# Division of softmax probabilities moved from VectorE to GpSimd in a two-layer streaming encoder

## The reference, cut to what matters

```python
def sink_softmax(s, sink):
    m = jnp.maximum(jnp.max(s, axis=-1, keepdims=True), sink)
    e = jnp.exp(s - m)
    return e / (jnp.sum(e, axis=-1, keepdims=True) + jnp.exp(sink - m))
...
    s = jnp.einsum('nbqhgd,nbkhd->nbhgqk', qb, kb).astype(jnp.float32) * ATTN_SCALE
    p = sink_softmax(s, sink)
    o = jnp.einsum('nbhgqk,nbkhd->nbqhgd', p.astype(v.dtype), vb)
```

## Time and profile before

| | before |
|---|---|
| median of 3 runs | 2451.64 us |
| profiled execution, its own time | 2451.63 us |
| span of that execution, first to last instruction | 2450.4 us |
| mean granted TensorE clock | 0.995 |
| busy: TensorE / VectorE / ScalarE / GpSimd | 2396.0 / 1652.9 / 842.4 / 109.6 us |
| chain that ended last, share of TensorE / VectorE | 92% / 4% |
| attention, first turn to last values, layer 0 | 209.42 to about 276 us |

### The profile page before, as it was taken

One profiled execution on the slowest core, in us unless ns is written; L12 is line 12 of the kernel. 1 busy time (PEld: TensorE's weight loads), 2 busy tenths in 40 slices (PEclk: granted clock), 3 DMA queues, 4 the chain that ended last, 5 costly groups with the idle time before them and its releaser, 6 DMA issues.

```text
span 2450.4 us, 45650 instructions
## 1 busy us (share of the span) xinstructions
PE 2396.0 (98%) x17474; PEld 2354.0 (96%) x17474; DVE 1652.9 (67%) x2472; ACT 842.4 (34%) x1602; POOL 109.6 (4%) x199
## 2 busy tenths in 40 slices
PE   6999999999999999999999999999999999999997
PEld 6997899999999999999999978999999999999996
DVE  8888888875435663645788888888754366556376
ACT  4126422223423432423431273222243244334243
POOL 0023100000000000000000231000000000000000
PEclk9999999999999999999999999999999999999998
DMA  4221122222232222222232201222222322222223
GB/s 182 86 86 37 36 84 85 79 78 78 95 98 87 78 86 78 77 86 78 88 122 79 94 19 60 77 86 77 81 83 92 102 86 78 85 78 86 78 82 105
DMA packets 57367, 204.22 MB, mean 83 GB/s; under 512 B 8142, under 2 KB 8238, under 8 KB 57006
## 3 DMA queue, kind: packets, MB, share of 16 engines
q1 hardware_dynamic: 52560, 190.03, 23.1%
q0 software_dynamic: 4704, 12.79, 1.8%
HBM read 193.14 MB, written 8.50 MB: 82 GB/s over the span
## 4 chain that ended last, share of the span: by engine, by line
PE 92%; DVE 4%; issue 1%; ACT 1%; DMA 0%; DVEq 0%; ACTq 0%; SPq 0%
PE ps L493 85%; PE ps L522 5%; PE ps L588 1%; DVE w_lo L1026 1%; ACT w_hi L760 1%; PE ps L573 1%; DVE scratch L1279 1%; PE ps L605 1%; PE ps L533 0%; DVE score_max L1252 0%; PE ps L590 0%; DVE scratch L1268 0%; DVE branch_lo L1287 0%; DVE scratch L1040 0%; DVE x_q_merged L1518 0%
## 5 line engine op out<-in xcount | busy, mean ns | idle before, releaser
L760 ACT ACTIVATE w_hi<-raw 128x1024 fp32r<-128x1024 f32 x348 | 368.9, 1060 | 1231.2 <-PE ps L493 1161.3
L493 PE MATMUL ps<-xn_hi,w_hi 128*128 128x296 f32 (+1 forms) x3584 | 779.1, 299 | 2.6 <-DVE w_lo L1026 2.6
L493 PE MATMUL ps<-xn_hi,w_lo 128*128 128x296 f32 (+1 forms) x3584 | 778.8, 299 | 0.0
L493 PE MATMUL ps<-xn_lo,w_hi 128*128 128x296 f32 (+1 forms) x3584 | 774.3, 297 | 0.0
L1026 DVE TENSOR_TENSOR w_lo<-raw,w_hi 128x1024 fp32r<-128x1024 f32 x350 | 428.7, 1225 | 494.1 <-ACT w_hi L760 493.0
L493 PEld LDWEIGHTS ps<-xn_hi,w_hi 128*128 128x128 f32 x3584 | 583.2, 189 | 4.3 <-DVE w_lo L1026 2.7
L493 PEld LDWEIGHTS ps<-xn_lo,w_hi 128*128 128x128 f32 x3584 | 582.8, 189 | 0.0
L493 PEld LDWEIGHTS ps<-xn_hi,w_lo 128*128 128x128 f32 x3584 | 579.8, 189 | 0.0
L493 PE MATMUL ps<-branch_hi,w_hi 128*128 128x296 f32 (+1 forms) x1296 | 282.7, 299 | 0.4
L493 PE MATMUL ps<-branch_hi,w_lo 128*128 128x296 f32 (+1 forms) x1296 | 281.6, 299 | 0.0
L493 PE MATMUL ps<-branch_lo,w_hi 128*128 128x296 f32 (+1 forms) x1296 | 279.9, 297 | 0.0
(11 more groups left out here) (160 smaller groups left out, 2173.3 us busy)
## 6 DMA issues: line engine op xcount, KB each, us to landing
raw<-in_weights SPq DMA_DIRECT2D x350, 512.0 KB, 3.2
spill<-x_q_merged POOLq DMA_DIRECT2D x2, 2368.0 KB, 9.3
x_q_merged<-spill POOLq DMA_DIRECT2D x16, 296.0 KB, 3.1
x_q_merged<-in_xt SPq DMA_DIRECT2D x4, 592.0 KB, 8.1
out_y<-x_q_merged SPq DMA_DIRECT2D x8, 296.0 KB, 2.3
scratch<-scratch POOLq DMA_DIRECT2D x64, 18.5 KB, 2.8
con<-in_consts SPq DMA_DIRECT2D x1, 592.0 KB, 11.3
vec<-in_vecs SPq DMA_DIRECT2D x1, 576.0 KB, 5.6
```

The lines of the kernel that those rows point to most:

```text
L493: last = nc.tensor.matmul(out[:, h, :], a[:, s, wk], b[:, k, t0 + h * n:t0 + (h + 1) * n], start=(k == 0 and j == 0), stop=(k == nk - 1 an ...
L760: nc.scalar.activation(wh[:, s, :], raw[:, s, :], ACT.Copy).then_inc(hi_done, 1)
```

## The change

The division leaves VectorE. GpSimd does it for all 20 units of a layer, in a new function `divide`, and its order becomes stage(0,0), stage(0,1), then for each chunk n: stage(n+1,0), divide(n,0), stage(n+1,1), divide(n,1). Each divide waits for its reciprocal and for the two copies ahead of it; each stage waits for the divide ahead of it. GpSimd's loop over the chunks is written out. On VectorE, denominators(n-1,1), now only the sum and the reciprocal, stands ahead of copy_rest(n-1,0), and the reciprocal waits until the division of the chunk before has read the old one. TensorE's transposes wait for the same semaphore as before, now raised by GpSimd. The nine DMAs after the last stage now also stand behind the last two divisions.

```diff
+            def divide(n, v):
+
+                nk = chunk_span(n)[2]
+                pool.wait_ge(rinv_done, l * 20 + n * 2 + v + 3)
+                pool.wait_ge(p_done, l * 20 + n * 2 + v + 3)
+                pool.wait_ge(qs_done, l * 20 + min(n * 2 + v + 3, 20))
+                plain()
+                probs = view(O_P + 768 * v, 768).rearrange("p (i n) -> p i n", i=4)[:, :, 0:nk]
+                nc.gpsimd.tensor_tensor(probs, probs, rinv[:, v, :].rearrange("p (i o) -> p i o", o=1)
+                                        .to_broadcast([128, 4, nk]), ALU.mult).then_inc(pn_done, 1)
+
+            for v in range(N_KV):
+                stage(0, v)
+            for n in range(CHUNKS):
                 for v in range(N_KV):
...
+                    if n + 1 < CHUNKS:
+                        stage(n + 1, v)
+                    divide(n, v)
...
-            pe.wait_ge(pn_done, it + 1)
+            pe.wait_ge(pn_done, it + 3)
...
             def denominators(n, v):
-                nk = chunk_span(n)[2]
                 it = l * 20 + n * 2 + v
                 dve.wait_ge(p_done, it + 3)
                 V.tensor_tensor(sums[:, v, :], sums[:, v, :], es[:, v, :], ALU.add).then_inc(den_done, 1)
                 dve.wait_ge(den_done, it + 1)
+                dve.wait_ge(pn_done, it + 1)
                 V.reciprocal(rinv[:, v, :], sums[:, v, :]).then_inc(rinv_done, 1)
-                dve.wait_ge(rinv_done, it + 3)
-                probs = view(O_P + 768 * v, 768).rearrange("p (i n) -> p i n", i=4)[:, :, 0:nk]
-                V.tensor_tensor(probs, probs, rinv[:, v, :].rearrange("p (i o) -> p i o", o=1).to_broadcast([128, 4, nk]),
-                                ALU.mult).then_inc(pn_done, 1)
...
                 if has(n - 1):
+                    denominators(n - 1, 1)
                     copy_rest(n - 1, 0)
-                    denominators(n - 1, 1)
```

More of the change, by code:

```diff
@@ L368, in plain @@
             nc.gpsimd.sem_inc(carrier, 1)
+        nc.gpsimd.sem_inc(pn_done, 2)
         pool.dma_start(vs[:, 0:WINDOW - DEC_SEQ, :], vcache[:, DEC_SEQ:WINDOW, :]).then_inc(vs_out, 16)
@@ L412, in _ @@
                     partners(m % 2)
-            def stage(c, n):
-                q0 = chunk_span(c)[0]
-                for v in range(N_KV):
[L418 to L434, removed]
+            def stage(n, v):
+                q0 = chunk_span(n)[0]
+                if n == 0:
+                    pool.wait_ge(qrot, l * KT + (4 * (v + 1) + 2))
+                pool.wait_ge(s_done, l * 20 + n * 2 + v + 1)
+                if n:
+                    pool.wait_ge(pn_done, l * 20 + n * 2 + v)
+                plain()
+                dst = view(O_QS + 512 * v, 512).rearrange("p (i n) -> p i n", i=4)
+                src = X[:, 4 * v:4 * v + 4, q0:q0 + 64]
+                nc.gpsimd.tensor_copy(dst[0:64, :, 0:64], src[0:64, :, :])
+                nc.gpsimd.tensor_copy(dst[64:128, :, 64:128], src[64:128, :, :]).then_inc(qs_done, 1)
```

## The result

The changed kernel takes 2460.12 us, median of 9 runs (2459.05 to 2463.84), against 2451.64 for the kernel before (9 runs). The ratio is 1.0039, 95% interval 1.0030 to 1.0047: slower by 8.5 us. The forecast was 2460, within 2450 to 2472, with 0.70 on slower.

What follows compares the result with a forecast made beforehand. TensorE was taken to wait for the division of a nearly full VectorE. Full-size steps 2.6 us and head 1.5 us gave 4.1 us a layer, 8.2 for two, on 2451.64: 2460 us, range 2450 to 2472.

Steps and rivals of the forecast that it cites:

- The bound before: Attention steps before the change: TensorE's own work 6.64 us, VectorE busy 6.93 of 7.20 us, its division keeping TensorE waiting.
- The price of the division: One GpSimd division of 768 elements per partition: 1.6 us taken, bounded by 0.8 and 2.34 us.
- two-pass figures: GpSimd division if each element costs two passes: 1.5 us at the fills' rate, 1.8 us at the copies' rate.
- The ring: Chain from a turn of group 1 through VectorE, GpSimd's division and stage, and TensorE to its next turn: 7.41 us a step.
- a branch behind: Path from group 0's division through turn(n,0) itself, in place of GpSimd's wait and stage copies: 0.16 us shorter.
- GpSimd's load: GpSimd's divisions and stage copies with its own waits in a steady step: 5.8 us.
- The lock: Port shared by VectorE and GpSimd, one holding the other off to its end: 0.1 us a step, making 7.51.
- Full-size steps: Six steps a layer growing from 7.08 to 7.51 us: 2.6 us more a layer.
- Head: Smaller chunks before the full-size steps, turns 0 to 3: 0.2, 0.2, 0.5 and 0.6 us later, 1.5 us a layer.
- Tail: End of a layer's attention: 2.8 us of other work covers the last 1.6 us division, DMAs come later; nothing.
- The reordering: On VectorE, sum and reciprocal of group 1 ahead of copy_rest(n-1,0): delays that copy 0.36 us, costed at nothing.
- the relief wins: Rival: VectorE emptied and a division below 1.17 us let TensorE's 6.64 us show; 2446 to 2447 us, chance 0.07.

Runs made afterwards that it cites:

- group 1 alone: Changed kernel, but only group 1's divisions on GpSimd, group 0's back on VectorE, new order of sums kept; 2447.93 us, ratio 0.9983 to the kernel before.
- the two with a repeated copy: Changed kernel with the first copy of every stage done twice, a wait between: in group 1 2475.00 us, in group 0 2462.99 us.
- the stages first: Changed kernel with GpSimd's order set to both stages ahead of both divisions; 2458.91 us, ratio 1.0020 to the kernel before.
- the early sum: Changed kernel, all divisions on GpSimd, VectorE taking sum and reciprocal of (n,0) before copy_rest(n-1,1); 2451.65 us, ratio 0.9997 to the kernel before.

## Why the prediction was right

Point by point, by its own steps.

- **The bound before.** TensorE at 6.64 us, VectorE ahead of it. The run with group 1 alone fits it: with VectorE at 6.08 the step is 6.65. But the load by itself isn't the bound. With the same divisions moved and VectorE's old order the step is 7.31, longer than before.
- **The price of the division**, 1.6 us taken, 1.5 to 1.8 its nearer bounds: measured 1.47. The sizes give 0.29, 0.72, 1.15 and 1.47 us for 64, 320, 576 and 768 elements, 1.7 ns an element and 0.2 fixed. That is the lower of the two two-pass figures. The 1.7 us estimated from the Trainium skill (GPSIMD Engine Reference, section 3.1) was 0.2 too high for this form, where one operand is broadcast; that this is the reason was not tried.
- **The ring**, 7.41 us: measured 7.34. The division is 0.13 shorter, GpSimd's wait for its own result 0.15 instead of 0.24, the copies 0.86 instead of 0.83, and the scores hold 0.09 more before the values start. That it is a ring, and that the stage lies in it with a branch behind that is 0.16 (measured 0.20) shorter, is shown by five runs together: the two with a repeated copy, the stages first, the early sum, and the division of group 1 alone. GpSimd's load, costed at 5.8 us with its own waits, is 7.34 - 2.14 = 5.2. The division of group 1 ends at 236.73, 0.8 us before its turn at 237.56, where 0.5 was forecast. VectorE was busy 5.48 us in its window of 7.40, where 5.2 was forecast; 0.2 of the difference is the small step of the maxima, below.
- **The lock** (the shared port), 0.1 us a step: in this kernel it costs next to nothing. The small step of maxima took 0.37 us at 233.63 and ended as GpSimd's division did (233.98), outside the ring, as the prediction's order of events had it. Inside the ring the copy at 234.13 took 0.42, 0.03 more than 0.39. The term was mis-sized by 0.07. The one meeting of long instructions that costs much, 0.76 us a step, was seen only with a division on each engine.
- **Full-size steps**, +2.6 us a layer: measured 43.98 - 42.49 = 1.5. **Head**, +1.5: measured 25.36 - 23.74 = 1.6 in layer 0, counted from the first scores. The parts came out otherwise, 0.33, 0.33, 0.46 and 0.50 for turns 0 to 3 where I had 0.2, 0.2, 0.5 and 0.6. **Tail**, nothing: so in layer 0. The sum of the ring and head is 3.1 us a layer, 6.2 in all, where I had 8.2.
- **The reordering**, costed at nothing: no cost, as argued, since VectorE had time. But it carries 3.4 us by the steps (12 x 0.28), for without it the division of group 1 isn't hidden. The medians give 6.5 (2466.63 - 2460.12) and the ratios some 4, with runs from 2461.28 to 2468.10. The prediction counted that division as hidden by 0.5 us without saying that this hangs on the new order.
- **What the prediction didn't have.** The profiled execution is 7.7 us longer, and the ring and head explain 6.1. Of the rest 1.6 us lie in the tail of layer 1 and 0.8 in the last four matmuls, both at the lower clock; against them the start was 0.75 us shorter. So the median met 2460 with two errors that cancelled: steps 2 us too long, and clock stretches left out. That the second holds for the median as it does for the profiled execution is not shown. The way of the change and the ring were forecast; that the median fell within 0.2 us of 2460 is luck.

The rival "the relief wins" named a division below 1.17 us as its condition; the measured 1.47 excludes it in this order. But the relief was there to be had in another way: 2447.93 us with group 1 alone, the fastest of all versions run.

## What to carry to other kernels

In this kernel taking work off a full engine paid only where the work's new place was outside the ring that closes once a step; add up that ring, through every engine and with each hand-over and what is queued behind the moved instruction, before looking at loads. Of two equal units of work, move the one whose result is needed latest: here group 1's division was free and group 0's cost 21 us more, about half of it by the ring and half because a copy in the ring met a division on VectorE. A reordering is judged together with the move: the same line cost time without it and saved time with it.

## What the runs showed of the hardware

TensorE's granted clock fell for short stretches that differ between executions. In the profile after, the tail of layer 1, and then a stretch of layer 0 that holds the same work (columns as above):

```profile
1486.90:1490.30 3.40, 3.40 (x17) 3.32 (x15) 1.01 (x2) 0.60 (x1) 3.40 (x5) 0.50 0.11 24
...
268.80:275.00 6.20, 5.38 (x40) 3.90 (x41) 1.71 (x5) 2.71 (x11) 5.38 (x7) 1.00 0.07 17
```

At 0.50 (1.2 GHz) for 3.4 us the tail took 1.6 us longer than before the change. TensorE's rows show what it did ahead of the stretch, and then the same product in it and behind it:

```profile
1484.61 1.08 PE L617 MATMUL ps<-scratch 96*64 96x256 f32 x8 [0.83 <-ACT scratch L891]
1486.51 0.33 PE L600 MATMUL ps<-con,scratch 128*128 128x128 f32 x1 [0.82 <-POOL scratch L437]
...
1488.42 0.68 PE L505 MATMUL ps<-xn_lo,w_hi 128*128 128x290 f32 x2
...
1493.88 0.43 PE L505 MATMUL ps<-xn_lo,w_hi 128*128 128x290 f32 x2
```

It had idled 0.83 and 0.82 us. Layer 0 has the same two idle times, and the clock stayed at 1.00; so these rows don't say by themselves when it falls. The product took 0.68 us at the lower clock and 0.43 at the higher. Such stretches of 3.4 to 10.2 us stand in the head or tail of attention in 7 of the 13 profiles. With group 1 alone one of 6.8 us made the way from turn(0,0) to turn(1,0) of layer 0 7.53 us, against 4.49 in layer 1; that profiled execution took 2451.51 us, the slowest of its 11. Adding up a ring doesn't show this cost. It goes with the spread of the times: of the 9 executions of the changed kernel the five from 2459.05 to 2460.12 have a mean granted clock of 0.993 to 0.995, the four from 2462.16 to 2463.84 one of 0.992 or 0.993. What makes the clock fall is not shown.
